# Where h, y and u lie in SBUF: bases at multiples of 2048 bytes, and h without gaps in the first block

## The reference

```
proj = rms_norm(x, ln1) @ w_in                     # 1024 -> 2824 columns
y    = concat(moba_attention, mlstm, swa_attention)
x    = x + y @ w_out
x    = x + square(relu(rms_norm(x, ln2) @ w_up)) @ w_down      # 1024 -> 4096 -> 1024
```

```
h    = modulate(rmsnorm(x, norm1), sh1, sc1); proj = h @ w_in
ret  = (silu(g) * head_rmsnorm(retention(q, k, v))) @ w_ret_o
pool = (grouped(causal_multiscale_pool(p)) * pool_scale) @ w_pool_o
x    = x + g1 * ((sigmoid(a_ret) * ret + sigmoid(a_pool) * pool) @ w_out)
h2   = modulate(rmsnorm(x, norm2), sh2, sc2); gate, up = split(h2 @ w_ffn_in)
x    = x + g2 * ((silu(gate) * up) @ w_ffn_out)    # 1024 -> 2 x 2816 -> 1024
```

## The kernel before

| tensor | before | above a multiple of 2048 | after |
|---|---|---|---|
| w_lo (over raw) | 16512 | 128 | 16512 |
| w_hi | 49280 | 128 | 49280 |
| h2 | 105856 | 1408 | 106496 = 52 x 2048 |
| y2 | 122368 | 1536 | 124928 = 61 x 2048 |
| u2 | 155008 | 1408 | 157696 = 77 x 2048 |

## Time and profile before

### The profile page before, as it was taken

The page is one execution under the profiler, slowest core; times in us unless marked ns, Lnnn a source line. Parts: engine busy times, 40 slices in busy tenths (PEclk is TensorE's granted clock), DMA queues, the critical chain, the costliest instruction groups (busy, mean ns, idle before and its releaser), DMA issues.

```text
span 1433.1 us, 25543 instructions
## 1 busy us (share of the span) xinstructions
PE 1407.3 (98%) x10339; PEld 1312.1 (92%) x10339; DVE 1145.7 (80%) x1799; ACT 828.5 (58%) x1249; POOL 10.5 (1%) x21
## 2 busy tenths in 40 slices
PE   8999999999999999999999999999999999999997
PEld 7898888889888888889999999998899999999986
DVE  7898888889798888887778777777777787778763
ACT  6776776445776875343666555444446575554542
POOL 2000000000000000000000000000000000000000
PEclk9999999999999999999999999999999999999999
DMA  9643999985445999987854578798787556778662
GB/s 257 161 140 92 284 266 268 299 229 163 137 140 169 278 259 295 284 248 217 226 153 144 172 233 233 212 250 231 225 235 217 148 147 180 231 208 232 180 186 64
DMA packets 485364, 297.13 MB, mean 207 GB/s; under 512 B 14956, under 2 KB 455792, under 8 KB 485120
## 3 DMA queue, kind: packets, MB, share of 16 engines
q1 hardware_dynamic: 483728, 292.00, 71.0%
q0 software_dynamic: 704, 1.66, 0.4%
q10 hardware_dynamic: 816, 1.84, 0.3%
HBM read 289.43 MB, written 1.05 MB: 203 GB/s over the span
## 4 chain that ended last, share of the span: by engine, by line
PE 77%; DVE 11%; ACT 6%; issue 3%; DMA 2%; SPq 1%; DVEq 0%; ACTq 0%
PE acc L1928 12%; PE acc L1929 12%; PE acc L1930 12%; PE mx L1945 9%; PE acc L1945 8%; PE mx L1946 5%; DVE w_lo L1073 4%; PE acc L1946 4%; DVE ada_acc L1163 2%; ACT w_hi L577 2%; PE acc L1960 1%; PE acc L1961 1%; PE acc L1962 1%; DMA rotb<-projb 1%; PE mx L2363 1%
## 5 line engine op out<-in xcount | busy, mean ns | idle before, releaser
L1073 DVE TENSOR_TENSOR w_lo<-raw,w_hi 128x1024 fp32r<-128x1024 f32 x450 | 541.5, 1220 | 113.3 <-ACT w_hi L577 111.4
L577 ACT ACTIVATE w_hi<-raw 128x1024 fp32r<-128x1024 f32 x450 | 458.2, 1049 | 137.7 <-DMA raw<-in_w_in 83.5
L1928 PE MATMUL acc<-h,w_hi 128*128 128x258 f32 (+1 forms) x1776 | 508.6, 286 | 8.4 <-DVE projb L1591 3.4
L1929 PE MATMUL acc<-h,w_hi 128*128 128x258 f32 (+1 forms) x1776 | 503.7, 284 | 0.0
L1930 PE MATMUL acc<-h,w_lo 128*128 128x258 f32 (+1 forms) x1776 | 498.0, 280 | 0.0
L1928 PEld LDWEIGHTS acc<-h,w_hi 128*128 128x128 f32 x1776 | 335.0, 189 | 15.7 <-issue 4.8
L1930 PEld LDWEIGHTS acc<-h,w_lo 128*128 128x128 f32 x1776 | 338.3, 190 | 0.0
L1929 PEld LDWEIGHTS acc<-h,w_hi 128*128 128x128 f32 x1776 | 335.9, 189 | 2.6 <-issue 2.4
L1945 PE MATMUL mx<-u,w_hi 128*128 128x512 f32 x864 | 303.4, 396 | 0.1
L1946 PE MATMUL mx<-u,w_lo 128*128 128x256 f32 x864 | 240.8, 279 | 0.0
L1945 PEld LDWEIGHTS mx<-u,w_hi 128*128 128x128 f32 x864 | 162.0, 188 | 37.1 <-DVE u L1877 0.4
(11 more groups left out here) (294 smaller groups left out, 1649.1 us busy)
## 6 DMA issues: line engine op xcount, KB each, us to landing
raw<-in_w_in SPq DMA_DIRECT2D x132, 512.0 KB, 4.0
ada<-in_w_ada SPq DMA_DIRECT2D x96, 512.0 KB, 5.0
raw<-in_w_ffn_in SPq DMA_DIRECT2D x88, 512.0 KB, 4.9
raw<-in_w_up SPq DMA_DIRECT2D x64, 512.0 KB, 5.6
raw<-in_w_down SPq DMA_DIRECT2D x64, 512.0 KB, 5.9
raw<-in_w_out SPq DMA_DIRECT2D x32, 512.0 KB, 3.9
raw<-in_w_ffn_out SPq DMA_DIRECT2D x32, 512.0 KB, 4.2
raw<-in_w_ret_o SPq DMA_DIRECT2D x16, 512.0 KB, 3.8
```

Of the source, the lines that this page charges most:

```text
L577: nc.scalar.activation(w_hi[:, n % NS], raw[:, n % NS], ACT.Copy).then_inc(hi_ready, 1)
L1073: V.tensor_tensor(w_lo[:, n % NS], raw[:, n % NS], w_hi[:, n % NS].bitcast(F32), ALU.subtract).then_inc(lo_ready, 1)
L1928: mm(outp, w_hi[:, i % NS, k], rhs[:, k, 0], start=k == 0, stop=False)
L1929: mm(outp, w_hi[:, i % NS, k], rhs[:, k, 1], start=False, stop=False)
```

## The change

Three unused tensors are put ahead of h, y and u, of 640, 1920 and 128 bytes, so that each of the three begins at a multiple of 2048. And in the first block (v below 4) h is used through a second view, `hd2`, of the same memory: rows of 256 numbers, high and low half of a tile next to each other, without the two unused columns. The second block reads and writes h as before, in rows of 258. No instruction is added, removed or moved on any engine.

```diff
+        sb("before_h2", [P, 160])
         h2 = sb("h2", [P, KT, 2, W], F32R)
+        sb("before_y2", [P, 480])
         with ExitStack() as beside_y:
...
+        sb("before_u2", [P, 32])
         with ExitStack() as mlp:
             u2 = sb("u2", [P, MLP_UP, 2, S], F32R, mlp)
...
-        (h_hi, h_lo), (y_hi, y_lo), (u_hi, u_lo) = [(t[:, :, 0], t[:, :, 1]) for t in (h2, y2, u2)]
+        hd2 = h2.rearrange("p k a w -> p (k a w)")[:, 0:KT * 2 * S].rearrange("p (k a s) -> p k a s", k=KT, a=2)
+        (h_hi, h_lo), (hd_hi, hd_lo), (y_hi, y_lo), (u_hi, u_lo) = [(t[:, :, 0], t[:, :, 1]) for t in (h2, hd2, y2, u2)]
+        hi_of = lambda v: hd_hi if v < 4 else h_hi
+        lo_of = lambda v: hd_lo if v < 4 else h_lo
...
-                nc.scalar.activation(h_hi[:, k, 0:S], xT[:, k], ACT.Copy, scale=gain(k)).then_inc(n_hi, 1)
+                nc.scalar.activation(hi_of(v)[:, k, 0:S], xT[:, k], ACT.Copy, scale=gain(k)).then_inc(n_hi, 1)
...
-                    nc.scalar.activation(h_hi[:, k, 0:S], xT[:, k], ACT.Copy, scale=ln2_of(l)(k)).then_inc(n_hi, 1)
+                    nc.scalar.activation(hd_hi[:, k], xT[:, k], ACT.Copy, scale=ln2_of(l)(k)).then_inc(n_hi, 1)
...
-                V.scalar_tensor_tensor(h_lo[:, k, 0:S], xT[:, k], gain(k), h_hi[:, k, 0:S].bitcast(F32),
+                V.scalar_tensor_tensor(lo_of(v)[:, k, 0:S], xT[:, k], gain(k), hi_of(v)[:, k, 0:S].bitcast(F32),
                                        ALU.mult, ALU.subtract).then_inc(h_ready, 1)
...
-            h_part = lambda k: h2[:, k, :, 0:S]
+            h_part = lambda k: hd2[:, k]
...
-                        slab(p0 + i, h2[:, :, :, 0:S], acc[:, i % 3, 0:S],
+                        slab(p0 + i, hd2, acc[:, i % 3, 0:S],
```

More of the change, by code:

```diff
@@ L768, in _ @@
                         act.wait_ge(x_ready, (2, 2, 4, 6)[k // 2])
-                        nc.scalar.activation(h_hi[:, k, 0:S], xT[:, k], ACT.Copy, scale=ln1_of(0)(k)).then_inc(n_hi, 1)
+                        nc.scalar.activation(hd_hi[:, k], xT[:, k], ACT.Copy, scale=ln1_of(0)(k)).then_inc(n_hi, 1)
                         if k == 3:
```

## The result

The changed kernel takes 1438.9 us (median of 6 runs, 1438.45 to 1440.77) against 1433.57 us of the kernel before, run with it: ratio 1.0041, with a 95% interval of 1.0028 to 1.0055. It is slower by 0.4%, about 5 to 6 us, and lies above the range of 1419 to 1437.5 us.

A forecast was written before the change was run, and what follows sets the result against it. TensorE's matmul pace was taken as the bound; 2.7 us (up slabs) plus 0.3 us (projection) plus nothing for the bases gave 3.0 us off 1434.96, or 1431.6 us as a median, range 1419 to 1437.5 us.

The forecast's parts named there:

- What bounds the kernel: Whole span: TensorE, busy 98%, bounds it through the pace of its matmuls; its longest wait is 3.4 us.
- The rows without gaps in the up slabs: First block's MLP up slabs: pace falls to u's, 5.2 ns a pair over 512 pairs, 2.7 us gained.
- The rows without gaps in the projection: First block's projection: reads become like y's, 0.24 ns for each of 1,104 matmuls, 0.3 us gained.
- The 109.2 ns: Skill's back-to-back figure, N/2.4 + 2.5 ns, for a 256-column matmul; set against y's 118.7 and left out of the sum.
- The bases, taken at nothing: h, y and u everywhere: starting at multiples of 2048 changes no pace, 0 us.
- The range that I gave for this part: Bases of h, y and u: from 17 us gained to 7 us lost.
- Rival S: Second block's 258-column h moves relative to the weights, surplus rises to 13.3 ns, 7.0 us lost; 1438.6 us; chance 0.11.
- Rival B: Place relative to the weights counts; u, up slabs and projection speed up, 6.6 us gained, 1428.0 us; chance 0.22.
- Rival C: Reads of h, y and u crossing a multiple of 2048 cost 3 ns a matmul; 20 us gained, 1414.6; chance 0.12.
- rival D: Layout means nothing to the reads; up and down slabs differ by PSUM tiles; 1434.6 us; chance 0.13.

The follow-up runs named there:

- experiment 1: Changed kernel without its three pads: old bases, rows without gaps in the first block kept; 1432.95 us, ratio 0.9996 to the kernel before.
- experiment 2: Kernel before plus the three pads: new bases, rows of h still 258 numbers in both blocks; 1439.12 us, ratio 1.0036.
- experiment 3: Changed kernel with weights and constants 128 bytes further on, h, y and u still at multiples of 2048; 1436.01 us, ratio 1.0021 to the kernel before.
- experiment 4: Changed kernel with h, y and u each 128 bytes further on, weights unmoved; 1438.27 us, ratio 1.003 to the kernel before.
- experiment 9: Changed kernel, bytes behind weights modulo 256: second block's h 0, first block's h 32, y 192, u 32; 1430.71 us, ratio 0.9983 to the kernel before.
- experiment 10: Kernel of experiment 9 with the first block's projection h at 192 instead of 32; 1428.79 us, ratio 0.9977 to the kernel before.
- experiment 13: Kernel of experiment 10 with y at 32 instead of 192 bytes behind the weights modulo 256; 1427.81 us, ratio 0.9967 to the kernel before.
- experiment 6: Changed kernel with other pads, bytes behind weights modulo 256: h 32, y 64, u 192; one execution, 1437.49 us.

## Why the prediction was wrong

**What bounds the kernel** was right: TensorE's pace, with small waits that the change left alone.

**The rows without gaps in the up slabs**, put at 2.7 us, gave 0.5 to 0.8 ns a pair, 0.3 to 0.4 us. I took u's 346.7 ns as the price of the contiguous form. It is the price of that form at place 0 only, and the lower of the two values that it has there. At the new place it costs 351.1, for u as for h. That the form by itself doesn't decide is shown by experiments 1 and 2: without the gap 2773 or 2830 at place 0, with it 2813; at place 128 the row with the gap is the faster one, 2787 against 2809.

**The rows without gaps in the projection**, put at 0.24 ns a matmul, came out so where slabs run undisturbed (2847 ns, 118.6 a matmul, against 118.9). It was right for the wrong reason: at h's old place the same rows cost 120.0 (experiment 1). The 109.2 ns that the prediction sets beside y's 118.7 was reached at no place: the fastest slabs take 113.3 ns a matmul.

**The bases, taken at nothing**, is the step that failed. The evidence was whether a read runs over a multiple of 2048, and that indeed doesn't matter: experiments 3 and 4 share all paces, with and without such a base. But the conclusion, that a move by a multiple of 128 bytes is neutral, did not follow. All rows of the trace before were at two places only, and each form of read stood at one of them, so no row could show what a form costs at the other. The range that I gave for this part held the answer, up to 7 us on the slow side, and the sum left it out. What the runs showed in its place: h in 258 columns went from 119.2 to 120.6 ns, 1.4 ns for each of 4,224 matmuls, 5.9 us; the bases alone give a ratio of 1.0036 and no bases 0.9996 (experiments 1 and 2).

**Rival S** is what happened in its main point: it named the second block's h, its distance to the weights and a surplus near 13.3 ns (it is 13.1), and a time of 1438.6 us. That the time is met within 0.3 us is luck: S took off 3.0 us for the rows without gaps, which gave about a third of that, had nothing for u and y, and counted from a median 1 us higher; the errors cancel. I gave it 0.11 with the argument that the move is a multiple of 128 and that h's rows drift by 16 bytes from k to k, so that the pace is an average over places. The table shows that the average still depends on the base: 2860, 2873, 2880, 2893 to 2907 and 2866 for 0, 32, 64, 96 or 128, and 192. **Rival B** had the period, 256 bytes, and the wrong sign: it compared y's pace with u's across two forms of read. Rival C is excluded by experiments 3 and 4, and rival D by the changed kernel itself, where up (acc) and down (mx) slabs have the same pace, so that the PSUM tile is not it.

**The sum of the loss.** 5.9 us in 176 slabs of 258 columns, 2 to 2.6 us on u, 0.6 us on y and the pool slabs, less 1.1 us by which the first block's projection and up stages are shorter, would be 7 to 8 us; 5 to 6 were measured. TensorE's waits were a little smaller in the profiled execution; whether that holds for the medians no run shows.

**Whose reads meet.** Experiment 3 moves the weights' buffers, which DMA, ScalarE and VectorE write while TensorE reads them. The end of both traces tells these apart. Behind 1406.9 us before and 1410.5 after, no engine writes `w_hi` or `w_lo` any more and the DMA share is 0.00, and the paces on u are still two different ones, 16 pairs at 346.9 and 351.3 ns (before, then after):

```profile
1407.00 0.39 PE L1945 MATMUL mx<-u,w_hi 128*128 128x512 f32 x1
...
1412.55 0.39 PE L1945 MATMUL mx<-u,w_hi 128*128 128x512 f32 x1
```

```profile
1410.64 0.40 PE L1951 MATMUL mx<-u,w_hi 128*128 128x512 f32 x1
...
1416.26 0.39 PE L1951 MATMUL mx<-u,w_hi 128*128 128x512 f32 x1
```

So it is not the writing of the weights that slows the reads of u. What these runs leave are TensorE's own two reads, of the moving operand and of the weights.

**What stays open.** How these two get in each other's way: the pace depends on their distance in steps of 32 bytes and, as far as tried, repeats after 256, but no row shows the reads themselves, so a collision of them is argued and not shown. Nor is it known what picks one of two paces at places 0, 32, 128 and 192, or whether it changes from one execution to the next, with one trace for each kernel; nor was any place between the multiples of 32 tried, nor 160 and 224. And no run shows why the time follows the paces only in part (experiments 4, 9, 10 and 13).

## What to carry to other kernels

Where the pace of matmuls is the bound and their operands are fp32r, the distance of the moving tensor from the weights' buffer modulo 256 bytes is a parameter that moved the pace of one form by up to 6% here (113.3 to 120.0 ns) and the time by 0.3% down or 0.6% up; it has to be tried for each form of read, and "aligned to 2048" is no help. An unrelated change of an allocation moves every tensor behind it and shifted the time by up to 0.6% here, so compare the paces of untouched stages before the change itself is credited. A pace gained is not yet time gained: about half of it was lost again in the fastest versions. And a row of one form of instruction at one place is no price for another form or place.

## What was not expected of the hardware

- The same 24 matmuls of 256 columns take 2720 to 2880 ns (113.3 to 120.0 ns each), by the place and by which of a place's two paces holds. Beyond the 106.7 ns that the prediction reckons for the columns alone, each takes 6.7 to 13.3 ns.
- At some places there are two paces: pairs on u at place 0 take 346.7 or 353.3 ns, plain slabs on y at 192 take 2720 or 2826. Stretches keep one until something interrupts the slabs: all changes in the down stages before and in experiment 3 stand at such an interruption. Which one it is differs between kernels whose tensor has the same address (u before and in experiment 1, the projection's h in experiments 6 and 9), and in experiment 1 between the first down stages of the two layers of one trace.
- The Trainium skill, TensorE: Matmul & The Clock Gate, Part 2, Step-by-step: what each phase is for, says that loading the next tile's weights doesn't take SBUF read bandwidth from the running matmul. Experiment 3, in which the weights moved and h, y and u did not, took the 258-column pace from 120.6 to 119.2 ns. For this stream of fp32r matmuls the pace therefore depends on how far the two operands lie apart, and the sentence does not hold here as it stands, unless something else than bandwidth joins the two reads, which no run shows.
